# A memory attention in high and low parts, its query and output projections laid between its steps

## The reference, cut to what matters

```python
def memory_cross_attention(q_in, m_in, w_q, w_kv, w_o):
    q = (q_in @ w_q).reshape(bsz, s, 4, 256)            # s = 512
    k, v = jnp.split(m_in @ w_kv, 2, axis=-1)           # 256 rows each
    scores = jnp.einsum("bshd,bmhd->bhsm", q, k)
    probs = jax.nn.softmax(scores * 256 ** -0.5, axis=-1)
    o = jnp.einsum("bhsm,bmhd->bshd", probs, v).reshape(bsz, s, 1024)
    return o @ w_o
```

## Time and profile before

| | us |
|---|---|
| median of 3 runs | 2302.94 (2302.93 to 2305.7) |
| the profiled execution, whole | 2302.18 |
| its span | 2300.4 |
| TensorE busy in it | 2227.1 |
| VectorE, ScalarE, GpSimd busy | 1265.5, 854.3, 326.6 |
| granted TensorE clock, mean | 0.985 |

### The profile page before, as it was taken

The page is one execution under the profiler, slowest core; times in us unless marked ns, Lnnn a source line. Parts: engine busy times, 40 slices in busy tenths (PEclk is TensorE's granted clock), DMA queues, the critical chain, the costliest instruction groups (busy, mean ns, idle before and its releaser), DMA issues.

```text
span 2300.4 us, 28121 instructions
## 1 busy us (share of the span) xinstructions
PE 2227.1 (97%) x11004; PEld 1767.8 (77%) x11004; DVE 1265.5 (55%) x1982; ACT 854.3 (37%) x1426; POOL 326.6 (14%) x324
## 2 busy tenths in 40 slices
PE   8899998989999999999999999999989999999998
PEld 7778787858888887776678888887875558888887
DVE  5765566354444445266645455455577874554554
ACT  4433454334222224355533222233255654222223
POOL 1300351001000003032210000001045541000001
PEclk9999999999999999999999999999988999999999
DMA  5233114403333332311123333333230003333331
GB/s 158 78 103 90 47 50 134 120 28 92 101 92 101 92 101 83 92 46 47 37 74 92 99 94 100 93 94 107 88 97 1 1 11 92 101 93 100 92 101 46
DMA packets 292659, 187.79 MB, mean 82 GB/s; under 512 B 7856, under 2 KB 286768, under 8 KB 292528
## 3 DMA queue, kind: packets, MB, share of 16 engines
q1 hardware_dynamic: 292240, 185.78, 27.0%
q10 hardware_dynamic: 288, 0.21, 0.0%
HBM read 183.88 MB, written 2.10 MB: 81 GB/s over the span
## 4 chain that ended last, share of the span: by engine, by line
PE 77%; DVE 3%; ACT 2%; issue 1%; POOL 0%; ACTq 0%; DVEq 0%; POOLq 0%
PE ps L469 75%; PE ps L503 2%; DVE tmp L2268 0%; DVE sb_small L2574 0%; ACT tmp L1530 0%; DVE nk_kwl L2301 0%; ACT ne_t L2525 0%; DVE sq L2269 0%; POOL acc L559 0%; DVE sb_small L1581 0%; DVE tmp L1587 0%; DVE sb_small L2577 0%; DVE xa_pt L1594 0%; ACT wh L455 0%; ACT tmp L2525 0%
## 5 line engine op out<-in xcount | busy, mean ns | idle before, releaser
L465 DVE TENSOR_TENSOR wl<-raw,wh 128x1024 fp32r<-128x1024 f32 x336 | 414.3, 1234 | 708.3 <-ACT wh L455 708.2
L455 ACT CAST wh<-raw 128x1024 fp32r<-128x1024 f32 x336 | 349.0, 1039 | 687.7 <-PE ps L469 672.1
L469 PE MATMUL ps<-xb_x,wh 128*128 128x512 f32 (+1 forms) x1488 | 461.9, 392 | 0.0
L469 PE MATMUL ps<-XH,wh 128*128 128x512 f32 x872 | 349.1, 400 | 9.7 <-issue 3.6
L469 PE MATMUL ps<-XH,wl 128*128 128x512 f32 x872 | 342.6, 393 | 0.0
L469 PE MATMUL ps<-XL,wh 128*128 128x512 f32 x872 | 342.2, 392 | 0.0
L469 PEld LDWEIGHTS ps<-xb_x,wh 128*128 128x128 f32 (+1 forms) x1488 | 277.9, 187 | 60.0
L469 PE MATMUL ps<-xb_x,wl 128*128 128x512 f32 (+1 forms) x744 | 291.8, 392 | 0.0
L559 POOL TENSOR_TENSOR acc<-acc,sq 128x512 f32<-128x512 f32 x55 | 76.1, 1383 | 1343.5 <-ACT sq L546 1342.2
L469 PEld LDWEIGHTS ps<-XH,wh 128*128 128x128 f32 x872 | 165.6, 190 | 47.2 <-issue 8.6
L469 PEld LDWEIGHTS ps<-XH,wl 128*128 128x128 f32 x872 | 165.3, 190 | 35.6
(11 more groups left out here) (352 smaller groups left out, 3494.3 us busy)
## 6 DMA issues: line engine op xcount, KB each, us to landing
raw<-in_mlp_w SPq DMA_DIRECT2D x128, 512.0 KB, 3.8
raw<-in_w_gate_up SPq DMA_DIRECT2D x44, 512.0 KB, 3.6
raw<-in_w_in SPq DMA_DIRECT2D x29, 512.0 KB, 3.6
raw<-in_sb_w_qkv SPq DMA_DIRECT2D x24, 512.0 KB, 3.7
raw<-in_w_down SPq DMA_DIRECT2D x22, 512.0 KB, 3.3
raw<-in_w_out_mix SPq DMA_DIRECT2D x16, 512.0 KB, 3.7
raw<-in_w_kv SPq DMA_DIRECT2D x16, 512.0 KB, 3.8
raw<-in_nsa_w_kv SPq DMA_DIRECT2D x12, 512.0 KB, 3.5
```

The lines of the kernel that those rows point to most:

```text
L455: e.copy(shaped(WH[i % NH], i), shaped(RAW[i % NR], i)).then_inc(*w_hi.up(i))
L465: e.tensor_tensor(shaped(WL[i % NH], i), shaped(RAW[i % NR], i), shaped(WH[i % NH], i).bitcast(F), ALU.subtract).then_inc(*w_lo.up(i))
L469: return e.matmul(out, a, b, start=start, stop=stop, skip_group_check=True)
```

## The change: what it does

- Keys, values, queries and turned probabilities are kept as high and low parts; a score group is then six products of 256 columns, a head's values twelve of 512. The queries lie in `X`, where the outputs follow head by head.
- The norm's sum and spread move up behind the second and third key unit; ScalarE's and VectorE's parts of it move with them.
- Only the query units 0 and 1 stand before the loop. Units 2 to 7 are computed in halves, one half in each step from -1 to 10, all in bank `NB`; VectorE scales the finished unit first thing in the next odd step.
- The loop uses six banks, `six`. In steps 16 and 17 the first four blocks of the output projections 0 and 1 are computed, in `PS[6]` and `NB`; after the values of head 3 come their blocks 4, 5 and then 6, 7.
- The turned block is copied (high part) by ScalarE and gets its low part on VectorE; VectorE's reciprocal and scaling of step n's exponential are issued in step n+1.
- The weight casts and their low parts follow the units into the loop.

The diff, cut to its core:

```diff
+    KT = Pair(ph.sb("kh", [128, 8, ML], R), ph.sb("kl", [128, 8, ML], R))
+    VT = Pair(ph.sb("vh", [128, 2, D], R), ph.sb("vl", [128, 2, D], R))
...
+    def xq_of(n):
+        u = 2 + (n + 1) // 2
+        return (u if u < 8 else None), (n + 1) % 2
+
+    def pv_at(n):
+        return (n - 7) // 4 if n >= 7 and n % 4 == 3 else None
...
     def plan_xattn():
...
+        six = Ring(PS[0:6])
+        for n in range(-1, 20):
+            u, half = xq_of(n)
+            if u is not None and half == 0:
+                plan(NB, ("xq", u), (v_made, ("xq", u)))
+                plan(sqr.next(), ("xqs", u), (x_lo, ("xq", u)))
+            if 0 <= n < 16:
+                plan(six.next(), ("xs", n), (a_made, ("xe", n)))
...
+            if 2 <= n < 18:
+                b = n - 2
+                plan(six.next(), ("xt", b), (x_lo, ("xpt", b)))
...
+            m = pv_at(n)
             if m is not None:
                 for j in range(2):
+                    plan(six.next(), ("xo", m, j), (x_lo, ("xo", 2 * m + j)))
+        plan(PS[6], ("xoo", 0), (h_new, ("xa", 0)))
+        plan(NB, ("xoo", 1), (h_new, ("xa", 1)))
...
     def pe_xattn(e):
         for o in range(8):
             t = take(e, ("mk", o))
             project(e, f"mk{o}", mp, "mem", t[:, 0:ML], ("mk", o), n=ML)
+            if o == 1:
+                pe_sum(e, "xa")
+            if o == 2:
+                pe_spread(e, "xa")
...
+        e.wait_ge(*x_lo.at("kT", 7))
+        e.wait_ge(*x_lo.at("vt", 1, 1))
+        pe_xattn_q(e, -1)
+        for n in range(20):
             if n < 16:
+                pe_xattn_scores(e, n)
+            pe_xattn_q(e, n)
+            if 2 <= n < 18:
+                pe_xattn_turn(e, n - 2)
+            if n in (16, 17):
+                pe_xattn_out(e, n - 16, 0, 4)
+            if pv_at(n) is not None:
+                pe_xattn_values(e, pv_at(n))
+        for o in range(2):
+            pe_xattn_out(e, o, 4, 6)
+        for o in range(2):
+            pe_xattn_out(e, o, 6, 8)
...
     def act_xattn(e):
...
+        for n in range(-1, 21):
+            u, half = xq_of(n)
+            if u is not None and half == 0:
+                act_weights(e, UI[f"xq{u}"] + 2)
+            if n % 2 and 1 <= n <= 11:
+                act_xattn_q(e, 1 + (n + 1) // 2)
+            if n == 13:
+                act_weights(e, UI["xo1"])
+            if 0 <= n < 16:
...
+            if 2 <= n < 18:
+                b = n - 2
+                P_ = take(e, ("xpts", b // 4)) if b % 4 == 0 else got(("xpts", b // 4))
+                e.wait_ge(*turned.at("xp", b))
+                e.copy(P_.hi[:, :, 128 * (b % 4):128 * (b % 4) + 128],
+                       got(("xt", b))[:, 0:256].rearrange("p (j t) -> p j t", j=2)).then_inc(*x_hi.up("xpt", b))
             if n >= 8 and n % 4 == 0:
+                h = (n - 8) // 4
+                for m in range(2):
+                    e.wait_ge(*mixed.at("xv", h, m))
+                    act_hi(e, X, "xo", 2 * h + m, got(("xo", h, m))[:, :])
...
     def dve_xattn(e):
...
+        for n in range(-1, 21):
+            u, half = xq_of(n)
+            left = 1 + (n + 1) // 2 if n % 2 and 1 <= n <= 11 else None
+            if left is not None:
+                dve_xattn_q(e, left)
+            if 0 <= n < 16:
...
+            if u is not None and half == 0:
+                dve_weights(e, UI[f"xq{u}"] + 2)
+            if n == 13:
+                dve_weights(e, UI["xo1"])
+            if left is not None:
+                dve_xattn_ql(e, left)
+            if 1 <= n < 17:
+                b = n - 1
...
+            if 2 <= n < 18:
+                b = n - 2
+                P_ = got(("xpts", b // 4))
+                hi, lo = (x[:, :, 128 * (b % 4):128 * (b % 4) + 128] for x in (P_.hi, P_.lo))
+                e.wait_ge(*x_hi.at("xpt", b))
+                e.tensor_tensor(lo, got(("xt", b))[:, 0:256].rearrange("p (j t) -> p j t", j=2), hi.bitcast(F),
+                                ALU.subtract).then_inc(*x_lo.up("xpt", b))
+            if n >= 8 and n % 4 == 0:
+                h = (n - 8) // 4
+                for m in range(2):
+                    dve_lo(e, X, "xo", 2 * h + m, got(("xo", h, m))[:, :])
```

More of the change, by code:

```diff
@@ L1454, in plan_xattn, with pe_xattn_q @@
-        for o in range(8):
+                    plan(six.next(), ("xo", m, j), (x_lo, ("xo", 2 * m + j)))
+        plan(PS[6], ("xoo", 0), (h_new, ("xa", 0)))
+        plan(NB, ("xoo", 1), (h_new, ("xa", 1)))
+        for o in range(2, 8):
             plan(psr.next(), ("xoo", o), (h_new, ("xa", o)))
         plan_next("ff")
+    def pe_xattn_q(e, n):
+        u, half = xq_of(n)
+        if u is None:
+            return
+        i = UI[f"xq{u}"]
+        t = take(e, ("xq", u)) if half == 0 else got(("xq", u))
+        e.wait_ge(*w_lo.at(i))
+        wh, wl = shaped(WH[i % NH], i), shaped(WL[i % NH], i)
+        for k in range(4 * half, 4 * half + 4):
+            mm(e, t[:, :], wh[:, k, :], XB.hi[:, k, :], k == 0, False)
+            mm(e, t[:, :], wh[:, k, :], XB.lo[:, k, :], False, False)
+            f = mm(e, t[:, :], wl[:, k, :], XB.hi[:, k, :], False, k == 7)
+        if half:
+            f.then_inc(*proj.up("xq", u))
+            if not proj.final:
+                proj.name("unit", i)
@@ new lines, in pe_xattn_out @@
+    def pe_xattn_out(e, o, k0, k1):
+        i = UI[f"xo{o}"]
+        t = take(e, ("xoo", o)) if k0 == 0 else got(("xoo", o))
+        e.wait_ge(*w_lo.at(i))
+        wh, wl = shaped(WH[i % NH], i), shaped(WL[i % NH], i)
+        for k in range(k0, k1):
+            e.wait_ge(*x_lo.at("xo", k))
+            mm(e, t[:, :], wh[:, k, :], X.hi[:, k, :], k == 0, False)
+            mm(e, t[:, :], wh[:, k, :], X.lo[:, k, :], False, False)
+            f = mm(e, t[:, :], wl[:, k, :], X.hi[:, k, :], False, k == 7)
+        if k1 == 8:
+            f.then_inc(*proj.up("xoo", o))
+            if not proj.final:
+                proj.name("unit", i)
@@ new lines, in pe_xattn_scores @@
+    def pe_xattn_scores(e, n):
+        h, i = XS[n]
+        t = take(e, ("xs", n))
+        e.wait_ge(*x_lo.at("xq", 2 * h + 1))
+        for kk in range(2):
+            o = 2 * h + kk
+            qh, ql = X.hi[:, o, 128 * i:128 * i + 128], X.lo[:, o, 128 * i:128 * i + 128]
+            mm(e, t[:, 0:ML], qh, KT.hi[:, o, :], kk == 0, False)
+            mm(e, t[:, 0:ML], qh, KT.lo[:, o, :], False, False)
+            f = mm(e, t[:, 0:ML], ql, KT.hi[:, o, :], False, kk == 1)
+        f.then_inc(*scored.up("xs", n))
@@ new lines, in pe_xattn_turn, with pe_xattn_values @@
+    def pe_xattn_turn(e, b):
+        t, p = take(e, ("xt", b)), got(("xp", b))
+        e.wait_ge(*v_made.at("xp", b))
+        turns(e, t, [(128 * j, 128, p[:, 128 * j:128 * j + 128], con("I")) for j in range(2)]).then_inc(
+            *turned.up("xp", b))
+    def pe_xattn_values(e, h):
+        P_ = got(("xpts", h))
+        e.wait_ge(*x_lo.at("xpt", 4 * h + 3))
+        for m in range(2):
+            t, cc = take(e, ("xo", h, m)), 2 * h + m
+            for j in range(2):
+                vh, vl = VT.hi[:, j, 128 * cc:128 * cc + 128], VT.lo[:, j, 128 * cc:128 * cc + 128]
+                mm(e, t[:, :], vh, P_.hi[:, j, :], j == 0, False)
+                mm(e, t[:, :], vh, P_.lo[:, j, :], False, False)
+                f = mm(e, t[:, :], vl, P_.hi[:, j, :], False, j == 1)
+            f.then_inc(*mixed.up("xv", h, m))
@@ L1472, in pv @@
[L1472 to L1482, removed]
@@ L1483, in pe_xattn @@
-        for n in range(18):
-            if n < 16:
[L1485 to L1499, removed]
@@ L1527, in act_xattn @@
[L1527 to L1531, removed]
+                if blk == 0 and kk == 0:
+                    e.wait_ge(*proj.at("mk", 7))
+                    act_hi(e, KT, "kT", 7, got(("mk", 7))[:, 0:ML], n=ML)
+            act_tokens(e, f"mv{blk}", lambda t: VT.hi[:, t, 512 * blk:512 * blk + 512], 512, 2)
@@ new lines, in act_xattn @@
+        for o in range(2):
+            act_weights(e, UI[f"xq{o}"] + 2)
+            act_xattn_q(e, o)
+        for n in range(-1, 21):
[7 more added lines that the diff above has]
+            if 0 <= n < 16:
+                w, pt = got(("xm", n)), take(e, ("xp", n))
+                e.wait_ge(*v_made.at("xm", n))
+                e.activation(pt[:, 0:ML], got(("xs", n))[:, 0:ML], ACT.Exp, bias=w[:, 1:2], scale=1.0 / 16,
+                             accum_out=w[:, 2:3]).then_inc(*a_made.up("xe", n))
+            if 2 <= n < 18:
[4 more added lines that the diff above has]
+                       got(("xt", b))[:, 0:256].rearrange("p (j t) -> p j t", j=2)).then_inc(*x_hi.up("xpt", b))
@@ L1547, in act_xattn, with dve_xattn_q, dve_xattn_ql @@
         a_.end("xa")
+    def dve_xattn_q(e, o):
+        t = take(e, ("xqs", o))
+        e.wait_ge(*proj.at("xq", o))
+        scaled(e, "xa", t[:, :], got(("xq", o))).then_inc(*v_made.up("xq", o))
+    def dve_xattn_ql(e, o):
+        e.wait_ge(*v_made.at("xq", o))
```

(22 more changed lines are left out.)

77 lines of the change are left out of this document (25 added, 52 removed).

## The result

The changed kernel takes 2297.96 us (median of 11 runs, 2296.47 to 2299.81), the kernel before 2302.94 (11 runs, 2299.1 to 2305.7). The ratio is 0.9981, 95% interval [0.9973, 0.999]: 5.0 us faster by the medians, 4.4 by the ratio, about the size of what can be told from no change. The profiled execution took 2296.93 us, its span is 2295.1; TensorE is busy for 2223.7 us of it.

What follows compares the result with a forecast made beforehand. TensorE, busy for 97% of the span, was taken as the bound. From the median 2302.94 us, -5.8 - 10.2 + 6.4 + 4.1 + 0.1 = -5.4 us gave 2297.5 us, with its own range 2295 to 2300.

Steps and rivals of the forecast that it cites:

- The products, -5.8: Scores and values in the memory attention: three products of high and low parts replace plain float32, saving 5.8 us of TensorE work.
- The old waits, -10.2: Loop of 18 steps: TensorE's 10.2 us of waits, mostly for VectorE's scaling of the probabilities, would go.
- The handovers, +6.4: Query units sharing one bank: TensorE waits for VectorE's scaling at n = 1, 3, 5, 7, 9; 6.4 us in all.
- Steps 11 to 15, +4.1: Late loop steps without a query half to hide behind: four waits of 0.6, 1.5, 1.0 and 1.0 us, 4.1 in all.
- The norm, +0.1: Keys' part: the norm's spread after mk2 is ready at 3.9 us, TensorE at 3.8; cost 0.1 us, at most 2.7.
- The prediction's sign of being right: Keys' part: TensorE would show no wait there but one under 0.3 us.
- The bank is free in time: Rival on the query bank: VectorE scales before the turn's low part, 6 us less, 2291.5 us; chance 0.13.
- Waits eat the gain: Rival: copies at their upper bound, 3 us, or a spread that isn't covered, 2.6: 2300 to 2302 us; chance 0.22.
- VectorE as the bound: Rival in the loop: the bank is released late at five handovers, 15 us over the forecast, 2312 us, slower; chance 0.07.
- That operations of VectorE pause: Rival: VectorE's operations don't overlap but pause for half their length, 3.5 us in all, 2301 us; chance 0.02.

Runs made afterwards that it cites:

- plain-products: Changed kernel, but scores and values are plain float32 products of the high parts alone, low parts left out of the products: 2302.24 us.
- queries-first: Changed kernel, but all eight query units stand before the loop again, so the loop scales no queries: 2301.47 us.
- two banks: Changed kernel, but query units 2 to 7 alternate between NB (even units) and PS[6] (odd units): 2291.57 us.
- the two experiments on it: Changed kernel with query units alternating between two banks, 2291.57 us; and, with one bank, VectorE scaling the finished query unit ahead of the low part, 2291.31 us.
- outputs last: Changed kernel, but output projections 0 and 1 are computed whole after head 3's values, nothing of them in steps 16 and 17: 2301.73 us.
- outputs spread: Against the two banks kernel: begun blocks of output projections 0 and 1 spread over steps 12, 13, 14, 16 and 17: 2288.44 us.
- norm one unit later: Changed kernel, but the norm's sum goes after the third key unit and its spread after the fourth: 2298.19 us.
- norm back: Changed kernel, but the norm's sum goes behind query unit 0, its spread behind unit 1, both queries scaled after it: 2299.23 us.
- scaling ahead: Changed kernel with one bank, but VectorE scales the finished query unit at the even step's end, ahead of the turned block's low part: 2291.31 us.

## Why the prediction was right

**The products, -5.8.** Right in size: a head's twelve products take 2.82 us where 2.73 was forecast, the six of a score group 0.71.

```profile
464.52 0.48 PE L469 MATMUL ps<-xp_h,xa_vh 128*128 128x512 f32 x1
...
467.34 0.28 PE L469 MATMUL ps<-xa_kh,XH 128*128 128x256 f32 x1
...
468.05 0.62 PE L469 MATMUL ps<-xb_x,wh 128*128 128x512 f32 x2
```

That they are on the path is shown by the plain-products kernel, less what the waits absorb: 4.3 between the medians, 4.6 worked out. The parts say the same: 174.19 without a fall, 171.37 less the 1.6 that its two falls cost (see below), a difference of 4.4.

**The old waits, -10.2.** Gone, as the loop's list of waits shows. That interleaving takes them off, not the new order of VectorE, is shown by queries-first: VectorE has the new order there, and TensorE stands idle for 9.1 us again, against 7.2 in the kernel before.

**The handovers, +6.4.** Measured 5.5 from start to start: 0.26 at n = 1 (0.3 predicted), three of 0.97 (predicted 1.2) and one of 2.3 (predicted 2.6). The mechanism is the predicted one, instruction by instruction, and is shown by undoing it in two ways. The size was off in two links: ScalarE's copy takes 0.37 us, not 0.41, and TensorE goes on 0.06 us after the scaling (443.86 + 0.68 = 444.54, then 444.60), not 0.15. The 0.15 came from a transpose after a VectorE write; for these products it was the wrong row.

**Steps 11 to 15, +4.1.** Four waits, in the places named. TensorE's order of time:

```profile
486.66 0.41 PE L503 MATMUL ps<-cst,tmp 128*128 128x128 f32 x2 [0.33 <-DVE tmp L1692]
488.18 0.38 PE L469 MATMUL ps<-xa_kh,XH 128*128 128x256 f32 x1 [1.11 <-DVE XL L496]
...
489.85 0.41 PE L503 MATMUL ps<-cst,tmp 128*128 128x128 f32 x1 [0.69 <-DVE tmp L1692]
```

With the start after each they cost 0.5, 1.3 and 0.9, where 0.6, 1.5 and 1.0 stood. The fourth, before turn 13, isn't there in this profile, since TensorE ran at half clock then. With two banks and no fall it is 0.64 us idle and costs 0.8:

```profile
485.84 0.44 PE L503 MATMUL ps<-cst,tmp 128*128 128x128 f32 x2 [0.64 <-DVE tmp L1692]
```

In all 3.4 without the fall.

**The norm, +0.1: the one step that was wrong in kind.** I took key units 1 and 2 to follow each other, though the earlier trace rows show 3.18 us of waiting before unit 2. The sum of squares falls in that gap and costs nothing (-0.8), and the road to the diagonals, which I had ending as TensorE comes, ends 0.85 us late: 0.60 idle before the spread in both repeats of the changed kernel, from the start of unit 2 to the spread 3.69 us for its 2.84. The prediction's sign of being right, no wait in the keys' part but one under 0.3 us, failed there. The two cancel, so the sum didn't suffer. First the profiled execution, then a row of the second repeat:

```profile
373.82 1.05 PE L469 MATMUL ps<-cst,acc 128*128 128x1 f32 x8 [0.63 <-POOL acc L559]
376.38 0.39 PE L469 MATMUL ps<-mm_mh,wh 128*128 128x256 f32 x1 [1.50 <-DVE wl L465]
...
377.77 0.41 PE L469 MATMUL ps<-mm_mh,wh 128*128 128x256 f32 x1
```

```profile
381.04 1.13 PE L469 MATMUL ps<-tmp,cst 128*128 128x128 f32 x8 [0.60 <-DVE tmp L593]
```

**What wasn't in the forecast.** The clock. The row at 377.77 has 0.41 where products of this shape have 0.28 at the full clock: from 377.2 to 380.5 us the products come 0.21 us apart instead of 0.12. Unit 2 takes 4.46 us (376.38 to 380.84) for 2.84. Of these 1.6 us 0.85 would have been the wait for the diagonals; a fall so placed costs 0.8. The late one costs as much: turn 12 to the end of the values is 5.58 us (489.85 to 495.43), and 4.80 with two banks and no fall (484.09 to 488.89); the latter holds the fourth wait, the former hides it.

Term by term the changed profile gives -5.8 - 10.2 + 5.5 + 2.7 (three late waits) - 0.8 (the sum in the gap) + 1.6 (first fall) + 1.7 (second, the fourth wait in it), which is -5.3 against 4.67 measured. The 0.6 left over is spread in small gaps between groups of different shape and I can't assign it. So two errors of opposite sign, waits priced 1.7 too dear and two unforeseen falls at 1.6 net, made the total better than its terms. That the forecast came within half a microsecond of the median is luck; either error alone would still have left the time in its range of 2295 to 2300.

**The rivals.** "The bank is free in time" is what the two experiments on it made true, at about the 6 us that it was priced at (6.4 and 6.7 between the medians, of which some 0.8 is one fall fewer in each profile). "Waits eat the gain" lost: ScalarE's copy took 0.37 us, near its lower bound, and VectorE's low part the 0.42 that the sum had; the spread cost 0.85 and not 2.6. VectorE as the bound is refuted by the two banks. That operations of VectorE pause is refuted by the handover's rows: 443.52 + 0.42 = 443.94, and the scaling starts at 443.86, before that. The Trainium skill ("VectorE: DVE Perf Modes", The DRAIN you can't avoid) says that the next operation doesn't start until the pipeline is empty, and adds that one which isn't held starts earlier. The prediction used the first half alone; here, as in the earlier trace rows, the measurement decides.

## What to carry to other kernels

Moving work between the steps of a latency-bound loop pays only as far as its own resources are handed over in time: here the interleaving took off 10.2 us of waits, one bank gave back 5.5 and the steps behind the moved work 3.4. An operation that is issued first in its step still stands behind the tail of the step before. When pricing such a loop, write down for each handover the whole in-order queue ahead of the releasing operation, from the last shared event on. And spread the filler to the steps that wait, rather than put it in two big pieces where waiting is nearly over: that was worth 2 us of waits (2291.57 to 2288.44 between the medians, the clock's 0.8 included; the intervals of the two ratios overlap by 0.0004).

## What the runs showed of the hardware

The granted clock stood at half, 1.2 GHz, for 3.4 us at a time, once for twice that, within a stage where it was 1.00 before. Each time TensorE had stood still shortly before, or stood still as it began: the 2.1 us of waiting before unit 2 (0.63 and 1.50), the 2.16 of the last handover, the 2.03 in the kernel before (and 2.02 at the same place with the outputs last and spread, outside the part), the 3.23 in queries-first, or the late waits of 0.33, 1.11 and 0.69. But the same waits passed without a fall in other executions: with plain products none of these places shows one, with two banks the late waits are the same and the late fall is missing, and the kernel before, with 7.2 us of waiting in its loop, had none behind that in three profiles. Its wait of 3.18 us before unit 2 had none behind it in the two profiles that hold it, but the same wait had one with the norm one unit later (3.17) and with the norm back (3.18). Near 490 us the fall came in all three executions of the changed kernel, and in all three experiments that keep its long bank waits and its products (norm later, outputs last, norm back); it is missing from the three profiles without these bank waits but with the interleaving (two banks, scaling ahead, outputs spread). That would fit the bank waits having a part in it, but queries-first has no bank waits and has the fall, and there is one profile of each: it is not shown. What decides it is open. It matters for reading: one profile's clock is not the kernel's, and a fall beside a wait costs only what the wait doesn't hide.
